# One level of Strassen in the first projection of a hybrid encoder step, with x transposed by the host and the side work moved to the second projection

## The reference, cut to what matters

```python
h = x * rsqrt(mean(x * x) + 1e-6) * g_pre          # RMS norm of each token
z = h @ w_in                                       # (tokens, 2048) @ (2048, 7760)
q, k, v, ga, qi, ki, wi, bg, cg, hc, gb = split(z)
# indexer: 16 heads score every admissible key, the 256 best keys of a query are kept
# attention over those keys, times silu(ga); short convolution of cg * hc, times bg * silu(gb)
y = x + rmsnorm(concat(attn, conv) @ w_out, g_post)
```

## Time and profile before

| | us |
|---|---|
| median of 3 runs (lowest, highest) | 2315.4 (2312.72, 2316.44) |
| the profiled execution | 2312.73 |
| its span, first to last instruction | 2310.9 |
| TensorE busy | 2220.0 (96%) |
| VectorE busy | 1013.0 (44%) |
| GpSimd busy | 759.8 (33%) |
| ScalarE busy | 707.2 (31%) |

### The profile page before, as it was taken

The page is one execution under the profiler, slowest core; times in us unless marked ns, Lnnn a source line. Parts: engine busy times, 40 slices in busy tenths (PEclk is TensorE's granted clock), DMA queues, the critical chain, the costliest instruction groups (busy, mean ns, idle before and its releaser), DMA issues.

```text
span 2310.9 us, 29863 instructions
## 1 busy us (share of the span) xinstructions
PE 2220.0 (96%) x12155; PEld 1978.3 (86%) x12155; DVE 1013.0 (44%) x1667; ACT 707.2 (31%) x994; POOL 759.8 (33%) x328
## 2 busy tenths in 40 slices
PE   5999999999999999999999999999999899999996
PEld 5999998999999999877777888887877788878885
DVE  5000005894361101355214879797885644342102
ACT  5121113322211124443324242424223634342221
POOL 4333332233333333222223434342432222233331
PEclk9999999999999999999999999999999999999998
DMA  4322232243222243344653333223232533265424
GB/s 165 106 90 104 100 115 70 90 93 105 79 83 87 79 145 114 131 133 122 184 166 128 126 103 101 96 96 112 98 115 82 176 120 100 91 230 198 152 76 191
DMA packets 160680, 274.65 MB, mean 119 GB/s; under 512 B 42656, under 2 KB 94880, under 8 KB 158624
## 3 DMA queue, kind: packets, MB, share of 16 engines
q1 hardware_dynamic: 160544, 272.74, 35.5%
HBM read 231.13 MB, written 41.56 MB: 118 GB/s over the span
## 4 chain that ended last, share of the span: by engine, by line
PE 83%; DVE 11%; issue 2%; ACT 2%; DMA 1%; DVEq 0%; SPq 0%; ACTq 0%
PE ps L916 57%; PE ps L947 17%; PE ps L967 4%; DVE isc L1534 2%; DVE top L1533 2%; PE ps L1012 2%; PE ps L873 2%; DVE isc L1521 1%; PE ps L1077 1%; DVE F L1580 1%; DVE act_lo L1353 1%; DVE F L1604 0%; DVE conv L1436 0%; DVE o_nat L1660 0%; DMA F<-in_x_prompt 0%
## 5 line engine op out<-in xcount | busy, mean ns | idle before, releaser
L845 POOL TENSOR_TENSOR w_lo<-w_raw,w_hi 128x1024 fp32r<-128x1024 f32 x308 | 745.3, 2420 | 1494.8 <-ACT w_hi L1106 1494.8
L916 PE MATMUL ps<-act_hi,w_hi 128*128 128x320 f32 (+1 forms) x2928 | 838.0, 339 | 6.3 <-DVE act_lo L1353 4.1
L916 PE MATMUL ps<-act_hi,w_lo 128*128 128x320 f32 (+1 forms) x2928 | 830.9, 337 | 0.0
L916 PE MATMUL ps<-act_lo,w_hi 128*128 128x320 f32 (+1 forms) x2928 | 830.6, 337 | 0.0
L1106 ACT ACTIVATE w_hi<-w_raw 128x1024 fp32r<-128x1024 f32 x308 | 326.2, 1059 | 773.7 <-PE ps L916 553.1
L916 PEld LDWEIGHTS ps<-act_hi,w_hi 128*128 128x128 f32 x2928 | 512.8, 189 | 49.6 <-issue 8.6
L916 PEld LDWEIGHTS ps<-act_hi,w_lo 128*128 128x128 f32 x2928 | 511.9, 188 | 39.7
L916 PEld LDWEIGHTS ps<-act_lo,w_hi 128*128 128x128 f32 x2928 | 512.6, 188 | 36.2
L947 PE MATMUL ps<-w_hi,act_hi 128*128 128x512 f32 x576 | 227.0, 394 | 9.2 <-issue 4.7
L947 PE MATMUL ps<-w_lo,act_hi 128*128 128x512 f32 x576 | 226.1, 393 | 0.0
L947 PE MATMUL ps<-w_hi,act_lo 128*128 128x512 f32 x576 | 225.9, 392 | 0.0
(11 more groups left out here) (159 smaller groups left out, 1500.9 us busy)
## 6 DMA issues: line engine op xcount, KB each, us to landing
w_raw<-in_w_in SPq DMA_DIRECT2D x244, 512.0 KB, 3.6
w_raw<-in_w_out SPq DMA_DIRECT2D x64, 512.0 KB, 4.1
qraw<-z_qi SPq DMA_DIRECT2D x24, 256.0 KB, 4.6
fin_x<-in_x_prompt SPq DMA_DIRECT2D x6, 1024.0 KB, 7.8
conv<-z_mix SPq DMA_DIRECT2D x16, 320.0 KB, 3.7
out<-o_nat SPq DMA_DIRECT2D x10, 512.0 KB, 3.1
F<-in_x_prompt SPq DMA_DIRECT2D x8, 512.0 KB, 5.7
qraw<-z_q SPq DMA_DIRECT2D x16, 256.0 KB, 3.0
```

What stands on the lines that cost most here:

```text
L845: nc.gpsimd.tensor_tensor(w_lo[:, r], w_raw[:, r], w_hi[:, r].bitcast(F32), ALU.subtract).then_inc(sem_w_lo, 1)
L916: last = nc.tensor.matmul(ps[:, bank + x, 0:w], wt[:, r, k % 8], a[:, k, w * x:w * (x + 1)], start=(k == 0 and wt is w_hi and a is act_hi) ...
```

## The change

**The projection of A by Strassen's scheme.** The contraction is cut in two halves and the 640 tokens in two halves of 320 (x11, x12, x21, x22); two tiles of weights are taken together (halves a11, a21 of the one, a12, a22 of the other). Seven products of 8 blocks by 3 parts, 24 matmuls of 320 columns each, take the place of eight. There are 30 pairs of tiles; the first tile (kiwi) stands alone and takes 4 products. Of the seven weight operands of a pair two are loaded halves and five are sums or differences of halves, which VectorE makes from `w_raw` (`weight_sum`); each is then split by ScalarE and GpSimd as before. VectorE adds up the seven results of a pair in `ev` with four copies by ScalarE and eight additions (`combine`, `pair_out`).

**x.** The host hands over x transposed (`x_a`, `x_b`). ScalarE scales it by `g_pre`; VectorE makes the sums of halves and all low parts (`scale_block`, `operand_sum`, `operand_low`). The 1/rms of the tokens is found apart from it (`squares`, `roots`, `broadcast_root`) and multiplied into the results of A (`finish`), and into x itself for B (`xb_scale`). The transposes of x are gone.

**Side work.** All steps that lay in the projection of A now lie in that of B: `timetable` starts at slot 8*61+2 and gives sections sizes in slots; heads of the next block run in one section with the rounds of the block before (two score buffers).

**Buffers.** `w_raw` gets 5 places (`RAW`), one `w_sum` is added, `act_hi` and `act_lo` hold 512 tokens, z of the last 128 tokens and the final loads are cut anew.

```diff
+RAW = 5
+HALF_A = T_A // 2
+NPAIR = (NP - 1) // 2
...
+SECTIONS = dict(heads2=10, rounds2=33, rounds3=48, softmax_a=65, streams=34, heads4=10, rounds4=48, rounds5=57, rounds6=64,
+                rounds7=76, last=16)
...
+    at = section(SLOTS * NP + 2, size["heads2"], [(("CHUNKS", 0), 1), (("CHUNKS", 1), 1), (("IK", "A"), 2)] + heads(2))
+    at = section(at, size["rounds2"], rounds(2), heads(3))
+    at = section(at, size["rounds3"], rounds(3), streams)
+    at = section(at, size["softmax_a"], softmax_steps("A", US_B), rounds("s"))
+    at = section(at, size["streams"], stream_softmax_steps())
+    at = section(at, size["heads4"], [(("IK", "B"), W["keys"])] + heads(4))
+    for b in (4, 5, 6):
+        at = section(at, size[f"rounds{b}"], rounds(b), heads(b + 1))
+    at = section(at, size["rounds7"], rounds(7), softmax_b[:cut])
+    at = section(at, size["last"], softmax_b[cut:half])
...
             def split_low(h):
-                if h < 2 * NT:
-                    pool.wait_ge(sem_w_hi, h + 1)
+                pool.wait_ge(sem_w_hi, h + 1)
+                r = h % RING
+                nc.gpsimd.tensor_tensor(w_lo[:, r], weight_source(h), w_hi[:, r].bitcast(F32), ALU.subtract
+                                        ).then_inc(sem_w_lo, 1)
...
+            def product(o, bank, u, start, stop, ready=None):
+                pe.wait_ge(sem_w_lo, o + 1)
+                for k in range(KT // 2):
+                    if ready is not None and k % CHUNK == 0:
+                        pe.wait_ge(sem_x_lo, 4 * READY[ready] + k // CHUNK + 1)
+                    for wt, parts in ((w_hi, (0, 1)), (w_lo, (0,))):
+                        for part in parts:
+                            last = nc.tensor.matmul(ps[:, bank, 0:HALF_A], wt[:, o % RING, k], xop[:, u, part, k],
+                                                    start=(start and k == 0 and wt is w_hi and part == 0),
+                                                    stop=(stop and k == KT // 2 - 1 and wt is w_lo))
...
+            def split_high(o):
+                if sums_through(o):
+                    act.wait_ge(sem_wsum, sums_through(o))
...
+                act.wait_ge(sem_gemm, max(o - RING + 1, 0))
+                copy(w_hi[:, o % RING], weight_source(o)).then_inc(sem_w_hi, 1)
+            def scale_block(name, u):
...
+                    for k in range(CHUNK * c, CHUNK * (c + 1)):
+                        last = nc.scalar.activation(xop[:, u, 0, k], raw_block[:, k], ACT.Copy, scale=g)
...
+                        last = nc.scalar.activation(raw_block[:, k], raw_block[:, k], ACT.Copy, scale=g)
...
+            def weight_sum(p, i):
...
+                if i == 1:
+                    dve.wait_ge(sem_w_lo, base - PAIR_OPS + 4 if p else 1)
+                    nc.vector.tensor_tensor(w_sum[:], buf["a11"], buf["a12"], ALU.add).then_inc(sem_wsum, 1)
+                if i == 3:
+                    dve.wait_ge(sem_w_lo, base + 2)
+                    nc.vector.tensor_tensor(w_sum[:], buf["a21"], buf["a22"], ALU.add).then_inc(sem_wsum, 1)
+                if i == 4:
+                    nc.vector.tensor_tensor(buf["a21"], buf["a21"], buf["a11"], ALU.subtract).then_inc(sem_wsum, 1)
+                    dve.wait_ge(sem_w_lo, base + 1)
+                    nc.vector.tensor_tensor(buf["a11"], buf["a11"], buf["a22"], ALU.add).then_inc(sem_wsum, 1)
+                if i == 6:
+                    nc.vector.tensor_tensor(buf["a12"], buf["a12"], buf["a22"], ALU.subtract).then_inc(sem_wsum, 1)
+            def combine(p, j):
...
+                nc.vector.tensor_tensor(out, out, ps[:, BANK[p, i], 0:HALF_A], op).then_inc(sem_cmb, 1)
+            def finish(p):
+                combine(p, 7)
+                if kind in ("k", "v", "qi", "q", "ga"):
+                    for u in range(2):
+                        nc.vector.tensor_tensor(ev[:, u], ev[:, u], rs_a[:], ALU.mult).then_inc(
+                            sem_ga_sc if kind == "ga" else sem_ev_rdy[u], 1)
+                elif kind == "cg":
+                    nc.vector.tensor_tensor(e0, e0, rs_a[:], ALU.mult)
+                    link(nc.vector.tensor_tensor(e1, e1, rs_a[:], ALU.mult))
...
                     nc.vector.memset(c_up[:, 0:2], 0.0)
                     nc.vector.tensor_copy(c_us[:, :, 0:2], st[:, c].rearrange("p (b j) -> p b j", b=NB))
+                    nc.vector.tensor_tensor(c_up[:, 2:514], e0[:, 0:512], e1[:, 0:512], ALU.mult)
+                    link(nc.vector.tensor_tensor(c_us[:, :, 2:18], e0[:, 512:T_A].rearrange("p (b t) -> p b t", b=NB),
+                                                 e1[:, 512:T_A].rearrange("p (b t) -> p b t", b=NB), ALU.mult))
                     nc.vector.tensor_copy(cs_s[:, c].rearrange("p (b j) -> p b j", b=NB), c_us[:, :, 16:18])
                     nc.vector.tensor_copy(u_prev[:, c], c_up[:, 512:514]).then_inc(sem_hc_rdy, 1)
+                    taps("A", c)
                 else:
+                    nc.vector.tensor_tensor(e1, e1, rs_a[:], ALU.mult).then_inc(sem_gb_sc, 1)
+                    link(nc.vector.tensor_tensor(e0, e0, rs_a[:], ALU.mult))
+                    link(nc.vector.tensor_tensor(c_y[:, 0:T_A], c_y[:, 0:T_A], e0, ALU.mult))
+                    dve.wait_ge(sem_gb_silu, c + 1)
+                    u, ready = RDY[pair_tiles(p)[1]]
+                    nc.vector.tensor_tensor(e0, c_y[:, 0:T_A], e1, ALU.mult).then_inc(sem_ev_rdy[u], 1)
...
+            for p in range(NPAIR):
+                for i in range(PAIR_OPS):
+                    if p and i == 0:
+                        finish(p - 1)
+                    for j in {3: (0,), 4: (1, 2, 3), 5: (4, 5), 6: (6,)}.get(i, ()):
+                        combine(p, j)
+                    if p or i + 3 >= 4:
+                        sums_ahead(FIRST_OPS + PAIR_OPS * p + i + 3)
...
+                    if p == NPAIR - 1 and i >= 3:
+                        for k in range(4 * (i - 3), 4 * (i - 2)):
+                            if k + 4 < KT:
+                                xb_scale(k + 4)
+                            xb_low(k)
```

More of the change, by code:

```diff
@@ L235, in timetable @@
[L235 to L244, removed]
@@ L245, in timetable @@
-    second = (("KK", "B", 1), ("QQ", 4, 1))
[L246 to L251, removed]
+    placed = []
@@ new lines, in section, with heads, rounds @@
+    def section(at, slots, *threads):
+        for steps in threads:
+            pos, total = at, sum(width for _, width in steps)
+            for step, width in steps:
+                placed.append((pos, len(placed), step))
+                pos += width * slots / total
+        return at + slots
+    def heads(b):
+        return [x for x in index_steps(b, US_B) if x[0][0] != "TK"]
+    def rounds(b):
+        steps = stream_index_steps() if b == "s" else index_steps(b, US_B)
+        return [x for x in steps if x[0][0] == "TK"]
@@ L252, in timetable @@
+    at = section(at, 4, [(step, 2) for step in second])
+    rest = wider(softmax_b[half:], W["so"])
+    at = section(at, sum(width for _, width in rest), rest)
+    assert at < SLOTS * (OUT_B - 1), at / SLOTS
+    section(SLOTS * (OUT_B + 1), 3 + 16 * 4, [(("RMS", "A"), 3)] + [(("FIN", i), 16) for i in range(4)])
+    side = {}
+    for pos, _, step in sorted(placed):
+        side.setdefault(int(pos), []).append(step)
     side[TAIL] = [("RMS", "B")] + [("FIN", i) for i in range(4, 9)]
@@ new lines, in broadcast_root @@
+            def broadcast_root(group):
+                pe.wait_ge(sem_x_dg, 1 + (group == "B"))
+                for j in range(5 if group == "A" else 4):
+                    name = ("rs", 2 if group == "B" else j // 4)
+                    if j % 4 == 0:
+                        bank_free(name)
+                    last = nc.tensor.matmul(ps[:, BANK[name], P * (j % 4):P * (j % 4 + 1)], ones,
+                                            diag[:, P * j:P * (j + 1)], start=True, stop=True)
+                last.then_inc(sem_rs_pe, 1)
@@ L920, in gemm @@
-                if s % 4 == 3 and n or n == 0 and s in (5, 7):
+                            last = nc.tensor.matmul(ps[:, bank, 0:T_B], wt[:, r, k % 8], a[:, k],
+                                                    start=(k == 0 and wt is w_hi and a is act_hi),
+                                                    stop=(k == KT - 1 and wt is w_lo))
+                if s % 4 == 3:
                     last.then_inc(sem_gemm, 1)
-                elif n in PHASE_LAST[:2]:
+                elif n == PHASE_LAST[1]:
@@ L934, in out_gemm @@
                         if use < 4:
-                            pe.wait_ge(sem_evac[use // 2], NP)
+                            pe.wait_ge(sem_evac[use // 2], sum(1 for x in range(NP, OUT_A) if x % 2 == use // 2))
                         elif pair < PAIRS:
```

1136 lines of the change are left out of this document (728 added, 408 removed).

## The result

The changed kernel takes 2423.3 us (median; 2416.6 to 2425.2), the one before 2315.9: a ratio of 1.046 (95% interval 1.044 to 1.048). That is 107 us slower, where 19 us slower was forecast, with a range up to 2380. The sign was right, the size was not.

The account below looks back on a forecast made before the run. The prediction took TensorE's chain of matmuls to bound the kernel. Its terms, 2310.9 - 61 (A) + 10 (into B) + 34 (side work) + 40 (waits) - 4 (rest), gave a span of 2330 us and a time of 2334 us; range 2256 to 2380.

Parts of the forecast that it names:

- 77 + 4 for waits: Projection of A: 77 us (43 to 103) of waits and held VectorE work, 4 for broadcasts and small transposes.
- signs of being wrong: Sums at 1.22 us and pairs of 24.7 us; A ending near 806; or weights waiting for DMA.
- one of the two works and the other is held: VectorE with both operands in SBUF and GpSimd exclude each other; projection of A 886 us with it, 806 without.
- GpSimd and VectorE miss each other: Rival, 20%: the two engines do not collide in the projection of A, which ends at 806; 2254 us in all.
- Together +40 (15 to 70): Projection of B: 14 to 22 us of waits in rounds4 to rounds7, plus 22 in rounds3 and softmax_a.
- the boundary: Into B: scalings and low parts of group B's x delay its first tile block by block, +10 us (5 to 15).
- a backlog of 8 us: Sections rounds4 to rounds7: VectorE's backlog of one head step, 8 us, costs nothing.
- The clock was a rival: Rival, 15%: waits behind cg or bg pairs halve the clock, 16 x 1.7 = 27 us; 2391 us in all.
- Its 30 us in the projection of B: Part of the rival on long waits: waits of B at their upper end, +30 us.
- The side work moved: TensorE's side work from the projection of A returns in full in that of B, +34 us.
- The term of -4 for the output projection of A: Side steps no longer cross into this output projection, where TensorE lost 4 us: -4 (0 to -10).

Follow-up runs that it names:

- The order: Changed kernel with the next block's, streams' or softmax's steps listed ahead of the rounds in sections rounds2 to rounds7: 2409.0 us (1.041).
- the sizes: Changed kernel with only the section sizes altered, such as rounds4 53 for 48 slots and last 13 for 16: 2393.3 us (1.034).
- the grain: Changed kernel with the rounds, the streams' too, in steps of one instead of two: 2402.0 us (1.038).

## Why the prediction was wrong

**The projection of A came out right, in part by luck.** It ends at 880.2, forecast 886 (870 to 905). The terms: the second pair begins at 97.3 instead of 90 (behind the first matmul at 19.6 TensorE waits 11.8 us up to 58 us, and 12.0 at 65); 29 pairs of 24.64; and 68.3 us instead of 77 + 4 for waits, with the plain pairs at nothing, cg at 3.6 and bg at 1.6 (forecast 0.5, 5 and 2.2). The 68.3 us hold some 17 us of lower clock that the sum did not have, and these make up for waits that were forecast too long. Two of the prediction's own signs of being wrong are there in the plain pairs: pairs of 24.64 us and, for four of the five sums, 1.22 us. What was held there were single instructions, a rescaling (3.02 us) or a low part of GpSimd's (up to 3.4 us), and no wait came of it. That one of the two works and the other is held was shown by taking GpSimd's part away and by giving it to VectorE. The rival 'GpSimd and VectorE miss each other' had 806 us; the projection ends at 804.4 when GpSimd's part is cut, close in the sum but not in its terms (the second pair begins at 84.3, not 78). The Trainium skill, "SBUF — State Buffer", section "Who interferes with whom", agrees, with 3.02, 1.08 and 0.82 us for one instruction beside it.

**The failed step is "Together +40 (15 to 70)" for the waits of the projection of B.** The idle time there, beside the boundary, is 106.3 us for 28.7: +78, just outside. In rounds4 to rounds7 I had set VectorE's 441 us against TensorE's 419 for the four sections as one and written off a backlog of 8 us. The runs show something else: VectorE is busy 415.9 us and TensorE 423.6, so VectorE has no excess at all, and yet the stretch takes 469.6 us, TensorE idles 46.0, not 14 to 22, and VectorE idles 53.7. Each section hands its lateness over at its end: the first head of the next one stands on VectorE behind what is left and two rounds, TensorE waits for all of it, and then VectorE waits for TensorE's head (20.3 of the 46.0 us at three heads; another 21.9 are softmax steps that wait for VectorE, most of them for F and pt_lo). Two engines that wait for each other in turn need more than the longer of them. In rounds3 and softmax_a TensorE idles 29.7 us, where I took 22; the other sections idle 30.6. The order (-14 us), the sizes (-30, of which 23 in this stage) and the grain (-21) each took a part of it, and leaving the rounds out took 68 us of 78.

**A term was missing: the pace.** The prediction carried 226.8 ns over to the changed kernel. The changed layout has 233.3 ns: 2928 x 6.5 = 19 us in the projection of B, and 12 in the output projections. Three places of one tile showed that it comes from where act begins.

**The clock was a rival and came in part.** After a wait of 3.63 us behind a cg pair, 96 matmuls took 1.8 us more than at 146.7 ns, with a granted clock of 0.58 in the first 4 us; the rival had 1.7 for each. Its 30 us in the projection of B were waits, not clock; there 24 us of busy time went with the rounds. By the starts of the pairs, a cg pair took 5.2 to 6.6 us over 24.64, so 1.6 to 3.0 beyond its wait, 17 in all; a bg pair, behind a wait of 1.6 us, only 0.2. The sum of A had room for that, since its waits were forecast too long. "HAM oscillation — how this bites in real kernels" in the Trainium skill's "TensorE: Matmul & The Clock Gate" describes such a loss behind waits; the rows agree for those of 3.6 us, and hardly show it behind those of 1.6.

**The rest.** The boundary is +17.1 us (forecast 10, 5 to 15): four scalings took 9.2 us beside GpSimd and 2.9 beside its short low parts, and the first tile of B does not wait block by block, as the prediction had it, but for an addition behind nearly all of VectorE's work on x. The side work moved was right at 34: by the starts of its matmuls TensorE's side products in B grew by 48 us, and those of the output projections shrank by 14. The term of -4 for the output projection of A failed: its first matmul, which waited 4.5 us before, waits 9.2. In the sum: -66.7 for A, 17.1, 78 of waits, 19 of pace, 48 of side work, some 12 that are left for the clock in B, and 4.5 behind it: 112 against 111.5 measured. Of the 92 us by which this exceeds the forecast of 19, 38 are waits, 19 pace, 14 side work from the output projections, 12 clock, 8.5 the end and 7 the boundary; A gave 6 back.

What stays open: the F waits (22 to 29 us in every run with all rounds, 5.7 without them), which neither order, sizes nor grain removed; what sets the 14.6 us of heads2 and heads4; why other sizes of the sections take away the wait of 9.2 us; and what the boundary becomes when the addition stands ahead of the work on x.

## What to carry to other kernels

When side work moves into a stage, do not weigh two engines' sums over the stage: write down at each hand-over what the late engine still has in its queue ahead of the instruction that the other one needs, and add these; then give the longer sections more slots and put that instruction first. The same holds where one stage ends: see what stands ahead of the instruction that frees the first PSUM bank of the next. If two engines hold each other for whole instructions, count their work as one; half of the conflict may vanish when the faster engine takes the slower one's part (2.41 us on GpSimd were 1.22 on VectorE). And when a change lays out memory anew, read the pace of the main loop again before anything else.

## What the runs showed of the hardware

The pace of long runs of 512-column matmuls depends on where their operands begin. With the weights at 128 by 512 bytes it is 226.8 ns when act begins at 128 or 384 by 512, 232.5 when act begins at 0, and 233.3 when act begins 32 behind a multiple of 64 (480 by 512). Whether the distance of the two or the place of act decides was not tested. (The softmax's groups of three, most behind a wait, show no such order: some 226 to 236 ns, mixed, in every run.) Runs of 320 columns kept 146.7 ns at every place. The granted clock shows nothing of it: it is 1.00 at 226.8 and at 233.3.
